# Self-attention with the probabilities as stationary operand and one division per block, sample stages and ffn steps in another order

## What is computed

```python
h = rmsnorm(x, norm_mix)
q, k, v, qi, ki, wi, glu = split(h @ w_in)
a = sparse_attend(...)    # 8 heads x 64; an indexer picks the 256 best keys per query; T5 relative bias
u = glu[..., :512] * sigmoid(glu[..., 512:])
c = silu(layernorm(causal_dwconv(u, conv_dw) + conv_db))      # 31 taps, 512 channels
x = x + concat(a, c) @ w_o
x = x + mem_attend(rmsnorm(x), mem_k, mem_v)                  # cross-attention, 4 heads x 64, 256 memory tokens
up = rmsnorm(x) @ w_up                                        # 2 * 2816 columns
g, val = split(causal_dwconv(up, ffn_dw) + ffn_db)            # 3 taps
x = x + (silu(g) * val) @ w_down
y = rmsnorm(x)
```

## Time and profile before

| what | value |
|---|---|
| time, median of 3 runs | 2092.79 us (2088.68 to 2094.74) |
| time of the profiled execution | 2086.14 us |
| its span on the core | 2084.3 us |
| mean granted TensorE clock | 0.889 |
| PE busy | 1772.0 us (85%) |
| PEld busy | 1568.5 us (75%) |
| DVE busy | 1274.8 us (61%) |
| ACT busy | 540.0 us (26%) |
| POOL busy | 703.0 us (34%) |
| read from and written to HBM | 92.49 MB and 16.00 MB |

### The profile page before, as it was taken

The page is one execution under the profiler, slowest core; times in us unless marked ns, Lnnn a source line. Parts: engine busy times, 40 slices in busy tenths (PEclk is TensorE's granted clock), DMA queues, the critical chain, the costliest instruction groups (busy, mean ns, idle before and its releaser), DMA issues.

```text
span 2084.3 us, 27921 instructions
## 1 busy us (share of the span) xinstructions
PE 1772.0 (85%) x10165; PEld 1568.5 (75%) x10165; DVE 1274.8 (61%) x2135; ACT 540.0 (26%) x1096; POOL 703.0 (34%) x399
## 2 busy tenths in 40 slices
PE   5399999978396998976968869999999999999984
PEld 3398899963252555656967859998999999999983
DVE  1555799999967889954464275534454363544466
ACT  4335511212121333322134134121122122112212
POOL 0412234259303258711300114343344334334430
PEclk9699999986686579998988679999999999999997
DMA  6311121213333000020100201111111111111102
GB/s 230 88 27 46 42 72 49 83 32 97 96 86 117 0 1 1 1 102 20 40 10 26 86 21 52 41 51 42 41 48 45 41 41 42 50 42 41 44 22 86
DMA packets 128873, 109.54 MB, mean 53 GB/s; under 512 B 10772, under 2 KB 110348, under 8 KB 128354
## 3 DMA queue, kind: packets, MB, share of 16 engines
q1 hardware_dynamic: 118597, 101.19, 16.0%
q10 hardware_dynamic: 10157, 6.67, 1.0%
HBM read 92.49 MB, written 16.00 MB: 52 GB/s over the span
## 4 chain that ended last, share of the span: by engine, by line
PE 60%; DVE 23%; issue 9%; ACT 3%; DMA 2%; SPq 1%; POOL 1%; DVEq 1%; ACTq 0%; POOLq 0%
PE ps L1569 42%; DVE hits L1240 4%; PE ps L1561 4%; PE ps L1586 3%; PE ps L1822 3%; PE ps L1853 2%; DVE conv_sum L1348 2%; DVE n_rstd L1133 1%; DVE n_rstd L1138 1%; PE ps L1802 1%; DVE th_keep L1244 1%; DVE up_conv L1513 1%; PE ps L1776 1%; DVE up_conv L1512 1%; DVE logits L1408 1%
## 5 line engine op out<-in xcount | busy, mean ns | idle before, releaser
L1569 PE MATMUL ps<-h_hi,w_hi 128*128 128x344 f32 (+1 forms) x1752 | 564.4, 322 | 30.9 <-DVE h_lo L1378 21.8
L1569 PE MATMUL ps<-h_hi,w_lo 128*128 128x344 f32 (+1 forms) x1752 | 562.0, 321 | 0.3
L1569 PE MATMUL ps<-h_lo,w_hi 128*128 128x344 f32 (+1 forms) x1752 | 561.7, 321 | 0.0
L647 POOL TENSOR_SCALAR w_hi<-w_raw 128x1024 fp32r<-128x1024 f32 (+1 forms) x107 | 118.3, 1105 | 1017.5 <-PE ps L1569 789.5
L1569 PEld LDWEIGHTS ps<-h_hi,w_hi 128*128 128x128 f32 (+1 forms) x1752 | 329.8, 188 | 35.5 <-issue 22.3
L1569 PEld LDWEIGHTS ps<-h_lo,w_hi 128*128 128x128 f32 (+1 forms) x1752 | 329.8, 188 | 2.4
L1569 PEld LDWEIGHTS ps<-h_hi,w_lo 128*128 128x128 f32 (+1 forms) x1752 | 330.0, 188 | 1.7 <-issue 1.1
L649 POOL TENSOR_TENSOR w_lo<-w_raw,w_hi 128x1024 fp32r<-128x1024 f32 (+1 forms) x107 | 287.8, 2690 | 8.9
L1531 DVE TENSOR_TENSOR xT<-xT,ps 128x344 f32<-128x344 f32 x264 | 135.3, 512 | 147.3 <-PE ps L1569 144.3
L1512 DVE SCALAR_TENSOR_TENSOR up_conv<-up,fw,up_conv 128x1024 f32<-128x1024 f32 x44 | 62.4, 1418 | 264.7 <-ACT upl L1088 264.7
L1569 PE MATMUL ps<-g_hi,w_hi 128*128 128x344 f32 x528 | 175.2, 332 | 36.1 <-DVE xT L1531 36.1
(11 more groups left out here) (324 smaller groups left out, 2784.4 us busy)
## 6 DMA issues: line engine op xcount, KB each, us to landing
w_raw<-in_w_up SPq DMA_DIRECT2D x44, 512.0 KB, 3.9
w_raw<-in_w_in SPq DMA_DIRECT2D x24, 512.0 KB, 3.8
w_raw<-in_w_down SPq DMA_DIRECT2D x22, 512.0 KB, 3.7
s_k_page<-in_cache_k SPq DMA_DIRECT2D x32, 256.0 KB, 2.9
s_v_pages<-in_cache_v SPq DMA_DIRECT2D x32, 256.0 KB, 3.0
x_spill<-xT SPq DMA_DIRECT2D x1, 4128.0 KB, 12.6
xT<-x_spill SPq DMA_DIRECT2D x1, 4128.0 KB, 13.5
x_tok<-in_x_prompt SPq DMA_DIRECT2D x2, 2048.0 KB
```

The lines of the kernel that those rows point to most:

```text
L647: pool.tensor_scalar(view(wh), view(wr), 1.0, 0.0, ALU.mult, ALU.add).then_inc(w_hi, 1)
L1569: mm = pe.matmul(out, view(w)[:, k, m0:m0 + m], x(k), start=(k == 0 and q == 0), stop=(k == ktiles - 1 and q == 2))
```

## The change

- The Toeplitz matmuls compute 256 columns; POOL fills the constant 128 with a memset.
- DVE does the sample's top-k and the sample convolution ahead of the masks, then masks of blocks 2 to 6, the sample softmax, and the mask of block 7. SP no longer waits for `masked` before K page 8; it does before the V pages of sample 3, which alone now lie where the masks work.
- The taps of tile 0 move into the attention loop: DVE does tile 0 at even items and tile 1 at odd ones, whole rows of 1024; POOL does all of tiles 2 and 3.
- PV in the loop has the transposed probabilities stationary (128 columns) and `v` moving (64 columns); the result has queries on partitions. Probabilities are not divided any more. Behind a block DVE divides the whole block's result by the sums (`nrm`), PE transposes it back (four transposes, `aT_n`), and ACT and DVE make high and low part from that, two items later than before.
- POOL's addition of the causal mask to `bt` goes (the constant in the Toeplitz rows does it).
- In the ConvFFN conv step 3 of group g + 1 comes behind the second half of `down(g)`.

```diff
-CUT_SOFTMAX = 8
-POOL_FIRST = 34
-POOL_AFTER_NB = {2: 1, 3: 1, 4: 2, 5: 3, 6: 3, 7: 2}
+POOL_FIRST = 36
+POOL_AFTER_NB = {2: 1, 3: 1, 4: 2, 5: 2, 6: 3, 7: 4}
...
-    yt0 = rxz.again(lg_at).take("conv_sum0", [P, S])
-    yt2 = rxz.again(u_at + 16896).take("conv_sum2", [P, S // 2])
+    r = rxz.again(u_at + 16864)
+    yt0 = r.take("conv_sum0", [P, S])
+    att_ = r.take("att", [P, DA])
+    assert r.at <= rxz.start + lg_at
...
-            if i == 2 * NPG:
-                sp.wait_ge(masked, 1)
-            if i % NPG == NPG - 1 and i // NPG < 4:
+            if i % NPG == NPG - 1 and i // NPG < 3:
                 v_pages(i // NPG)
+        sp.wait_ge(masked, 1)
+        v_pages(3)
...
+        pool.memset(tst[:, :, 2 * P:3 * P], NEG).then_inc(tst_ok, 1)
...
-            w = S // 2 if m == 2 else S
+            w = S
...
-        pool.tensor_tensor(bt[:, :, P:2 * P], bt[:, :, P:2 * P], causal[:, :].unsqueeze(1).to_broadcast([P, NH, P]),
-                           ALU.add).then_inc(bt_ok, 1)
-        pool.wait_ge(bt_ok, 1)
         pool.wait_ge(masked, 1)
...
-            act.activation(tst[:, h, :], ps[:, 5 + h % 2, 0:384], ACT.Copy).then_inc(tp_c, 1)
+            act.activation(tst[:, h, 0:2 * P], ps[:, 5 + h % 2, 0:2 * P], ACT.Copy).then_inc(tp_c, 1)
         act.wait_ge(tp_c, NH)
+        act.wait_ge(tst_ok, 1)
...
-                if i >= 2 * NH:
-                    act.wait_ge(scaled, i - 2 * NH + 1)
+                if h == 0 and b >= 2:
+                    act.wait_ge(nrm, b - 1)
...
-            if i >= 12 and (i - 12) % 8 == 0:
-                b = (i - 12) // 8
-                act.wait_ge(pv, NH * (b + 1))
+            if i >= 14 and (i - 14) % 8 == 0:
+                b = (i - 14) // 8
+                act.wait_ge(aT_n, b + 1)
...
+        def pre_masks():
+            sample_top_k()
+            by_tile = cw[:, :].rearrange("p (j m) -> p m j", m=CT)
+            for m in range(CT):
+                mm = dve.tensor_tensor(us[:, m, :, :], us[:, m, :, :], by_tile[:, m, :].unsqueeze(1).to_broadcast([P, DB, CW]), ALU.mult)
+            self_.link(mm)
...
+        pre_masks()
         for b in BIG:
...
+            if b == NB - 2:
+                sample_softmax()
         dve.sem_inc(masked, 1)
...
-        def taps(j0, j1):
-            with dve.Fori(j0, j1) as j:
-                for e, cols in enumerate(halves):
-                    dve.wait_ge(tap, 2 * j + (e - 1))
-                    dve.scalar_tensor_tensor(out=yt0[:, cols], in0=u[:, 0, bass.ds(j + S // 2 * e, S // 2)],
-                                             scalar=cw[:, bass.ds(CT * j, 1)], in1=yt0[:, cols],
-                                             op0=ALU.mult, op1=ALU.add).then_inc(tap, 1)
...
-        taps(1, CUT_SOFTMAX)
-        sample_softmax()
-        taps(CUT_SOFTMAX, HALO)
-        for e, cols in enumerate(halves):
-            dve.wait_ge(tap, 2 * (CW - 1) - 1 + e)
-            dve.scalar_tensor_tensor(out=y[:, 0, cols], in0=u[:, 0, cols], scalar=cw[:, 0:1], in1=yt0[:, cols],
-                                     op0=ALU.mult, op1=ALU.add).then_inc(tap, 1)
         sample_heads()
-
-        def tap_of(m, t0, n, acc, done, k):
+        dve.wait_ge(ksm_out, 32)
...
-                    dve.wait_ge(bt_ok, 1)
+                    dve.wait_ge(bt_in, 16)
...
-            if 1 <= i < len(ITEMS) + 1:
-                n = i - 1
-                b, h = ITEMS[n]
-                dve.wait_ge(exp_ok, n + 1)
-                self_.link(dve.reciprocal(ri[:, b % 2, h:h + 1], rs[:, b % 2, h:h + 1]))
-                row_ = lg[n % 3][:, 0:P * (b + 1)]
-                dve.tensor_scalar(row_, row_, ri[:, b % 2, h:h + 1], None, ALU.mult).then_inc(scaled, 1)
...
-                tap_of(1, 0, S, yt1, tap1, i // 2)
+                tap_of(0, yt0, tap0, i // 2)
             if i % 2 and i // 2 < CW:
-                tap_of(2, S // 2, S // 2, yt2, tap2, i // 2)
-            if i >= 13 and (i - 13) % 8 == 0:
-                b = (i - 13) // 8
+                tap_of(1, yt1, tap1, i // 2)
+            if i >= 12 and (i - 12) % 8 == 0:
+                b = (i - 12) // 8
+                dve.wait_ge(exp_ok, NH * (b + 1))
+                self_.link(dve.reciprocal(ri[:, b % 2, :], rs[:, b % 2, :]))
+                dve.wait_ge(pv, NH * (b + 1))
+                if b >= 1:
+                    dve.wait_ge(aT_n, b)
+                heads = att_[:, :].rearrange("p (h d) -> p h d", h=NH)
+                dve.tensor_tensor(heads, ps[:, 6 + b % 2, :].rearrange("p (h d) -> p h d", h=NH),
+                                  ri[:, b % 2, :].unsqueeze(2).to_broadcast([P, NH, DH]), ALU.mult).then_inc(nrm, 1)
+            if i >= 15 and (i - 15) % 8 == 0:
...
                 down(g, 0, unit0)
+                down(g, 1, unit0)
                 conv(g + 1, 3)
-                down(g, 1, unit0)
...
-            pe.matmul(ps[:, 5 + h % 2, 0:384], rbx[:, h, :], toep[:, :], start=True, stop=True).then_inc(tp_t, 1)
+            pe.matmul(ps[:, 5 + h % 2, 0:2 * P], rbx[:, h, :], toep[:, 0:2 * P], start=True, stop=True).then_inc(tp_t, 1)
...
-                pe.wait_ge(scaled, n + 1)
+                pe.wait_ge(exp_ok, n + 1)
...
-                half = 64 * (h % 2)
                 for k in range(b + 1):
-                    mm = pe.matmul(ps[half:half + DH, 6 + b % 2, h // 2 * P:(h // 2 + 1) * P], v_[:, k, h * DH:(h + 1) * DH],
-                                   pt[n % 2][:, k, :], start=(k == 0), stop=(k == b))
+                    mm = pe.matmul(ps[:, 6 + b % 2, h * DH:(h + 1) * DH], pt[n % 2][:, k, :], v_[:, k, h * DH:(h + 1) * DH],
+                                   start=(k == 0), stop=(k == b))
                 mm.then_inc(pv, 1)
-
-
-        pe.wait_ge(tap, 2 * CW)
+            if i >= 13 and (i - 13) % 8 == 0:
+                b = (i - 13) // 8
+                pe.wait_ge(nrm, b + 1)
+                for m in range(CT):
+                    mm = tr(ps[:, 6 + b % 2, m * P:(m + 1) * P], att_[:, m * P:(m + 1) * P])
+                mm.then_inc(aT_n, 1)
```

103 lines of the change are left out of this document (44 added, 59 removed).

## The result

The changed kernel takes 2110.54 us in the median of 17 executions (2089.32 to 2113.83), the kernel before 2090.6 in 17 beside it; the ratio is 1.0068, 95% interval 1.0044 to 1.0092. It is slower by some 20 us on the median and by 14 us on the mean, from which the ratio comes: 11 of the 17 took 2109 to 2114 us, 6 took 2089 to 2098. The profiled execution, one of the 11, took 2112.24 us, 26.1 more than that of before. The forecast was +29 us. The time lies in the range, but the difference of the medians is two thirds of the one forecast and that of the means half of it, and behind it two terms of the sum were off by 16 and 17 us in opposite directions.

The account below looks back on a forecast made before the run. The attention loop was taken as bound by TensorE at 1.2 GHz first, VectorE later. Terms -3.5 - 28 + 99 + 1.5 - 40 = +29 us gave 2115 for the profiled execution, 2122 on the median's scale; range 2050 to 2145.

Parts of the forecast that it names:

- Part 3: Attention loop: all eight blocks at 1.2 GHz, TensorE bounding throughout, 357.3 us against 258.6: +99 us, and +1.5 behind it.
- Part 2: Sample stages ahead of the attention loop: VectorE's new order starts the loop at 625 instead of 653.2, -28 us.
- Toeplitz, -3.5: Toeplitz matmuls: 256 instead of 384 columns take a third less of 10.57 us on the path; bounds 0 and -3.5.
- Sample stages, -28: Before the attention loop: top-k and sample conv ahead of the masks, `masked` at 591, loop start at 625; bounds -24 and -33.
- Loop, +99: Attention loop: 1.07 us per key tile plus 0.66 per item at 1.2 GHz, 357.3 us against 258.6; bounds -9 and +6.
- The row that the clock was forecast from: Cross-attention's sample stage: TensorE and loads busy 12.00 of 12.00 us at clock 0.50, so loads do not restore the clock.
- VectorE no longer bounds, POOL is hidden: Attention loop: VectorE falls to some 3 to 3.6 us per item; the 4 `tap_step` moved on POOL cost nothing.
- Tail, +1.5: Behind the loop: division, transposes, high and low part before the layer norm's sums, two more hops; bounds 1 and 4.
- ffn, -40: ConvFFN: moving the conv step saves 4.9 us in each of nine groups, less in the tenth: -40 us, bounds -35 and -44.
- rival C: Attention loop: the upper clock comes back only in block 6; sum -35.5, 2057 us, faster; chance 0.08.
- its own sign of being wrong: Attention loop: a clock of 1.00 anywhere in blocks 4 to 7, or VectorE still full there, would refute the forecast.
- Rival B: Attention loop: the upper clock comes back in block 4; loop 249.5 us, sum -79, 2014 us, faster; chance 0.18.

Follow-up runs that it names:

- run with bursts at blocks 4 to 7: Changed kernel plus six extra, overwritten 128x512 matmuls before the first PV of each of blocks 4 to 7; 2052.59 us, ratio 0.9824.
- run with bursts of loads: Changed kernel plus fourteen extra matmuls of 128 stationary, 64 moving columns before the first PV of blocks 4 to 7 each; 2158.94 us, ratio 1.0309.

## Why the prediction was right or wrong

The sign, the mechanism and the main term's cause were right: in the profiled execution the loop ran at 1.2 GHz but for its last 6.3 us, TensorE without a gap from block 3 on, and the new PV with its division does it. The size was wrong: +29 was forecast, and measured were +26.1 between the profiled executions, +20 between the medians and +14 between the means. Three steps failed. In Part 3 the item's fixed part was taken over from the old form, 0.66 us, where 0.35 was measured: 20 us too much, and the step that puts the forecast above the measurement. In Part 2 the masks of blocks 2 to 6 were priced without the full width of POOL's operations: the stage gave 12 us and not 28. And the clock was taken as low in every execution; six of 17 were some 17 us faster. Of the 15 us between the forecast and the means, 3 are what is left of the sum's errors, which nearly cancel; 7 come from the faster executions of the changed kernel, and 5 from the kernel before, whose profiled execution was that much faster than the mean of its 17. Step by step:

- **Toeplitz, -3.5.** The matmuls fell from 10.57 us to 7.16, as said, but the next product of the memory tokens started at 60.08 instead of 60.97 and the indexer's pages at 459.05 instead of 459.43: 3 of the 3.4 us were covered by a later wait. "On the path" was wrong; the lower bound, 0, was right.
- **Sample stages, -28: a step that failed.** Measured -12 between the profiled executions. (Two kernels with this stage as before started their loops at 656.2 and 656.5 instead of 653.2, and the changed one once more at 639.2 instead of 641.2, so it may be -17; the step fails with either.) The masks of blocks 2 to 6 were priced at 42.9 us, before's time under POOL's taps; they took 55.9. The multiplication by the sign ahead of them took 12.04 us instead of 6.33, so that top-k could start only at 506.2, and top-k and the sample convolution took 31.6 instead of 28.9. The text had noted that tile 2 on POOL becomes full width, and charged it nothing but for block 7. Block 7's mask was over-priced instead (13.7 against 7.7, for POOL had ended). `masked` came at 604 and not 591, the loop started at 641 and not 625. Halving the width gives 13.5 us back, taking POOL away 19.4.
- **Loop, +99: a step that failed in its size.** Measured +81.7. The clock, and TensorE as the bound, were right. With the new PV the item's fixed part is about 0.35 and not 0.66: the transposes take 0.69 us at three tiles up to PV's start instead of 0.83, and PV 1.31 instead of 1.47. 64 items at 0.31 less are 20 us. Why they follow each other more closely was not tested. PV itself at 0.43 a tile, where 0.42 was taken, gives 3 back: 357.3 - 19.8 + 2.9 = 340.4, for 340.3 measured (343.3 in the second profile).
- **The row that the clock was forecast from.** In the cross-attention's sample stage "nearly all time is loads with 4 moving columns" was read too strongly. The timeline shows that stretch as 1.6 us of them and then 0.9 us of transposes with 128 moving columns, over and over: behind the eight records at 1143.28 come four transposes at 1144.85 (L1561) and the next eight at 1145.73. The forecast of the clock held, on weaker ground than was said.
- **VectorE no longer bounds, POOL is hidden:** right (28.42 of 53.9 us in block 5, 26.67 for POOL).
- **Tail, +1.5:** right.
- **ffn, -40:** -45.7 in the changed kernel, a little beyond its bound of -44. Between kernels with the same count of transfers on the instruction queue it is -36 to -41, inside the bounds; the other 7 to 10 us come with the smaller count, which nobody forecast. The gap before the last down-projection is 8.62 us; "some 10" was said.
- **The forecast's one number.** It took the clock as low or high for a whole case. Measured, the late rise is neither rival C nor absent: it comes in some executions only, in block 7 where a profile caught it, and takes 13 to 22 us off them (2089 to 2098 against 2111). By its own sign of being wrong, a clock of 1.00 anywhere in blocks 4 to 7, the prediction met it at the very end of block 7.
- **Rival B (a rise in block 4)** did not come by itself. The run with bursts at blocks 4 to 7 shows that its price for the loop was good: 273.9 us less 23 for the bursts is 251, where 249.5 was reckoned (with block 7 at 0.604 x 8 x 8 + 0.8 = 39.5 and not 37.5, it is 251.5). Its total of 2014 was missed by 39 us through the bursts and the late start.

Two errors of 16 and 17 us cancelled each other, by luck: with the sample stages alone set right the sum would have been +45, with the loop alone set right +12.

## What to carry to other kernels

Before an operand swap, ask which clock the loop will run at, not only what the swap costs per instruction: of two forms with the same time per instruction, one had the upper clock for most of the time from block 4 on and the other stayed at 1.2 GHz, 72 to 83 us apart, and 23 us of wide matmuls took 58 us off. Where POOL and VectorE run beside each other, price VectorE's short instructions by the length of POOL's single operations, and keep those narrow or elsewhere in time. And price parts alone before bundling: here everything but the swap was worth -46 us, and the swap took it all back. When two kernels differ in a stage that no edit touched, look at the counts of the queues before explaining the total.

## What had not been expected

- **Superfluous matmuls that pay.** 24 matmuls of 512 columns without use took 58 us off, and only the first 12 of them met the low clock.
- **Narrower POOL operations let VectorE through.** 36.2 us for the masks in halves is below the 42.9 of the kernel before, though there tile 2 was of the same width; there steps of tile 3, full width, began at 528.7 while masks ran.
- **A gap in a loop from nowhere near.** In the run with bursts of loads the ConvFFN took 756.7 us from the first up-projection to the start of the last down-projection's second half, against 730.5 in the changed kernel run once more, with no edit there. The timeline of TensorE shows a pair of gaps in it, the second put down to "issue", which means that nothing in the profile held it:

```profile
1510.52 0.42 PE L1548 MATMUL ps<-h_hi,w_hi 128*128 128x344 f32 x1 [1.07 <-DVE xT L1510]
1513.41 0.32 PE L1548 MATMUL ps<-h_lo,w_hi 128*128 128x344 f32 x1 [2.47 <-issue]
```

The pair comes four times, 141 to 143 us apart, once for each further pass of the loop over two groups, each time with 2.2 to 2.8 us of "issue". The eight gaps are 14.5 us, and behind each pair the clock reads 0.50 for 3.4 or 6.8 us. The run has 45 transfers on the instruction queue in this stretch, against 9: nine more in each further pass. The six other kernels with 45 have the first gap of the pair, 0.8 to 1.4 us in each of those passes, the kernels with 9 have neither, and no other run has a second one of more than 0.3 us. So the first gap goes with the transfers; that they cause it, and why the second comes in this run only, stays open. Some 24 us of that run's total are not the bursts'.
